# A three-block transformer in fp32: the first stage reordered by need, its norm sums on VectorE, head norms with two root and two square buffers

## The reference

```python
for l in range(2):                                   # first_block
    mod  = silu(c) @ w_ada[l] + b_ada[l]             # six groups of 1024: sh1 sc1 gt1 sh2 sc2 gt2
    modc = silu(c_ctx) @ w_ada[l] + b_ada[l]
    h = rmsnorm(x, g_mix[l]) * (1 + sc1) + sh1       # the same for ctx with modc
    p = h @ w_in[l]
    # q and k heads of 64: rmsnorm of each head, gain, then rotation t*cos + turned(t)*sin
    x = x + gt1 * mixer(...)    # global and windowed attention, short convolution, gates, w_out
    x = x + gt2 * expert_choice_ffn(...)             # 16 experts, each takes its top tokens
# second_block: rmsnorm, q/k/v/gate projections, head norm and rotation, banded and
# dilated causal attention, silu gates, w_out, residual
```

## Time and profile before

| | us |
|---|---|
| median of 3 runs (lowest to highest) | 3480.6 (3479.9 to 3485.0) |
| the profiled execution's own time | 3479.7 |
| its span in the trace | 3477.7 |
| PE busy | 3198.9 (92% of the span) |
| DVE busy / ACT busy | 1075.6 / 641.6 |

### The profile page before, as it was taken

One profiled execution on the slowest core, in us unless ns is written; L12 is line 12 of the kernel. 1 busy time (PEld: TensorE's weight loads), 2 busy tenths in 40 slices (PEclk: granted clock), 3 DMA queues, 4 the chain that ended last, 5 costly groups with the idle time before them and its releaser, 6 DMA issues. The chain is left out here.

```text
span 3477.7 us, 35357 instructions
## 1 busy us (share of the span) xinstructions
PE 3198.9 (92%) x13776; PEld 1568.4 (45%) x13776; DVE 1075.6 (31%) x1541; ACT 641.6 (18%) x1124; POOL 16.7 (0%) x35
## 2 busy tenths in 40 slices
PE   6989999999997999999988999999789889888978
PEld 3565555555553333333343654444423324343544
DVE  2566644555422010101036561011300010036241
ACT  3137500000011111111121560000111101021151
POOL 1000000000000000000000000000000000000000
PEclk8999999999998999999999999999899999999999
DMA  7020033443414878787830201223198988942200
GB/s 222 0 73 1 1 121 115 145 150 105 139 49 154 304 285 307 285 304 289 303 93 0 73 1 55 73 73 103 37 376 346 404 355 352 405 114 49 61 1 25
DMA packets 305434, 551.85 MB, mean 159 GB/s; under 512 B 62744, under 2 KB 145960, under 8 KB 305160
## 3 DMA queue, kind: packets, MB, share of 16 engines
q1 hardware_dynamic: 303376, 546.53, 44.2%
q0 software_dynamic: 1600, 3.20, 0.3%
q10 hardware_dynamic: 312, 0.05, 0.0%
HBM read 547.63 MB, written 2.10 MB: 158 GB/s over the span
## 5 line engine op out<-in xcount | busy, mean ns | idle before, releaser
L736 PE MATMUL ps<-hT,ring 128*128 128x512 f32 (+1 forms) x2576 | 969.6, 534 | 29.5 <-ACT hT L1259 27.7
L736 PEld LDWEIGHTS ps<-hT,ring 128*128 128x128 f32 x2576 | 492.6, 192 | 494.1 <-issue 464.4
L1013 PE MATMUL ps<-ring,hT 128*64 128x512 f32 x1536 | 356.9, 600 | 64.4 <-DMA ring<-in_w_e_up 35.5
L992 PE MATMUL ps<-ring,hT 128*64 128x512 f32 x1536 | 350.8, 598 | 1.5 <-ACT hT L1259 1.5
L1013 PEld LDWEIGHTS ps<-ring,hT 128*64 128x64 f32 x1536 | 100.2, 136 | 311.1 <-issue 159.3
L1906 DVE SCALAR_TENSOR_TENSOR xT<-ps,mod,xT 128x512 f32<-128x512 f32 x96 | 63.5, 662 | 498.7 <-PE ps L1099 281.1
L992 PEld LDWEIGHTS ps<-ring,hT 128*64 128x64 f32 x1536 | 101.8, 136 | 235.6 <-issue 235.1
L736 PE MATMUL ps<-obuf,ring 128*128 128x512 f32 (+1 forms) x512 | 198.5, 540 | 1.3 <-issue 1.3
L998 PE MATMUL ps<-ring,hT 128*32 128x512 f32 x1536 | 184.7, 598 | 0.0
L1591 DVE SCALAR_TENSOR_TENSOR vbuf<-ring,silc,vbuf 128x1024 f32<-128x1024 f32 x140 | 179.9, 1285 | 5.7
L1259 ACT ACTIVATE prob<-ps 128x512 f32<-128x512 f32 (+1 forms) x56 | 38.6, 688 | 673.7 <-PE ps L736 673.7
(11 more groups left out here) (223 smaller groups left out, 2471.0 us busy)
## 6 DMA issues: line engine op xcount, KB each, us to landing
ring<-in_w_e_gate SPq DMA_DIRECT2D x128, 512.0 KB, 7.2
ring<-in_w_e_up SPq DMA_DIRECT2D x128, 512.0 KB, 7.1
ring<-in_w_e_down SPq DMA_DIRECT2D x128, 512.0 KB, 6.9
ring<-in_w_e_gate SPq DMA_DIRECT2D x64, 1024.0 KB, 10.6
ring<-in_w_e_up SPq DMA_DIRECT2D x64, 1024.0 KB, 10.7
ring<-in_w_e_down SPq DMA_DIRECT2D x64, 1024.0 KB, 10.7
ring<-in_w_in SPq DMA_DIRECT2D x49, 1024.0 KB, 5.6
ring<-in_w_ada SPq DMA_DIRECT2D x48, 1024.0 KB, 6.8
```

The costliest lines, as they stand in the source:

```text
L736: mm = pe.matmul(ps[:, b + a:b + e], lhs[:, k, :], rhs[:, k, a:e], start=k == 0, stop=k == nk - 1)
L992: mm = pe.matmul(ps[e * CX:(e + 1) * CX, b + pair * 512:b + (pair + 1) * 512], lhs[:, k, s0:s0 + CX], expert_dst(0, slot, e)[:, k % 2, :], ...
L1013: mm = pe.matmul(ps[e * CX:(e + 1) * CX, b + h * 512:b + (h + 1) * 512], lhs[:, k, s0:s0 + CX], expert_dst(1, slot, 0)[:, e, h * 512:(h + ...
```

## The change

1. SP: the big block of constants (rotation, head and mask tables) is issued after the eight `w_ada` chunks and two `w_in` chunks; the identity matrix stays in front. c and c_ctx have their own small DMAs, first on ACT's queue, and are turned ahead of x.
2. The eight `w_ada` chunks are cut otherwise: 256 rows by 1024 columns in place of 1024 rows by 256 columns. Four chunks make one group: sc1 (`adf` g=1) first, then sh1 (g=0), each copied and turned once.
3. ACT squares each tile of x as soon as it is copied; DVE adds the eight squares up (`add_square`); PE needs one product over 768 columns (job `ns`) in place of eight. Root and reciprocal follow between the two groups.
4. DVE scales by the root alone; the amplitude goes into ACT's shift operation (`scale=`). Both go through the 512 columns of all `d` first, then the 256, in all layers; PE waits for each range apart, and so does the reciprocal.
5. The meetings of all engines in the first stage are gone.
6. Head phase, all layers: two root buffers, two square buffers, a scratch of its own for the rotation, and the rotation one job later.

```diff
-C_ID, C_SUM, C_PICK, C_ROT, C_HEAD, C_MASK, C_IOTA = 0, 128, 130, 134, 262, 390, 390 + 7 * P
+C_ID, C_PICK, C_ROT, C_HEAD, C_MASK, C_IOTA = 0, 128, 136, 264, 392, 392 + 7 * P
...
+        cond = pr[0:2 * KD, 2, 0:P]
+        roots = [rs, pr[:, 1, :]]
+        squares = [sq, pr[:, 2, :]]
+        turn_term = pr[:, 0, 0:NX]
...
                 order.append(j)
-                if rots:
+                if len(rots) > 1:
                     order.append(rots.pop(0))
...
-        FIRST = [(w, 0, n + (w == "ada")) for n in range(-1, 8) for w in ("ada", "adat") if 0 <= n + (w == "ada") < 8]
+        FIRST = [("adf", 0, 1, q) for q in range(4)] + [("ns", 0), ("adft", 0, 1)]
+        FIRST += [("adf", 0, 0, q) for q in range(4)] + [("adft", 0, 0), ("pv", 1)]
...
-            if name == "ada":
-                return plain(w_ada[l], n * CH)
-            if name == "acc":
+            if name in ("adf", "acc"):
...
                     for k in range(nk):
-                        if ph is not None and (ph, k) not in seen_h:
-                            need(h_ready, ph + (k,))
-                            seen_h.add((ph, k))
+                        if ph is not None and (ph, k, a) not in seen_h:
+                            need(h_ready, ph + (k, a))
+                            seen_h.add((ph, k, a))
...
+                elif kind == "ns":
+
+                    pe.wait_ge(first_added, 1)
+                    b = begin(("norm", 0, "mix"))
+                    for a, e in halves(NT):
+                        mm = pe.matmul(ps[:, b + a:b + e], ones[:, :], h3[:, 0, a:e], start=True, stop=True)
+                    part(mm, ("norm", 0, "mix"))
...
+            pe.wait_ge(s_ident, 16)
+            pe.wait_ge(s_cond, 32)
+            b = begin(("cond", 0))
+            part(pe.transpose(ps[:, b:b + 2 * KD], cond, ident[0:2 * KD, 0:2 * KD]), ("cond", 0))
             pe.wait_ge(s_x, 32)
-            pe.wait_ge(s_const, 32)
...
-            sp.dma_start(con[:, 0:C_ROT], consts[:, 0:C_ROT]).then_inc(s_const, 16)
+            sp.dma_start(con[:, 0:C_ROT], consts[:, 0:C_ROT]).then_inc(s_ident, 16)
...
+            for n in range(RING + 4):
+                load(n)
             sp.dma_start(con[:, C_ROT:C_HELD], consts[:, C_ROT:C_HELD]).then_inc(s_const, 16)
-            end = 0
+            end = RING + 4
...
                 elif kind == "qk":
                     w = width(l, j[2])
+                    n = hs_number[("hs",) + j[1:]]
                     b = A.read(j)
-                    if last_hs[0]:
-                        A.read(last_hs[0])
-                    A.do(func(sq[:, 0:w], ps[:, b:b + w], ACT.Square), qsq_ready, j)
-                    last_hs[0] = ("hs",) + j[1:]
+                    if n >= 2:
+                        A.read(hs_of[l][n - 2])
+                    elif l > 0:
+                        A.read(("affT", l - 1))
+                    A.do(func(squares[n % 2][:, 0:w], ps[:, b:b + w], ACT.Square), qsq_ready, j)
                 elif kind == "hs":
-                    A.need(*last_rs[0])
-                    root(j, width(*j[1:]), HD)
-                elif kind == "rot":
-                    last_rs[0] = (q_ready, j)
+                    n = hs_number[j]
+                    if n >= 2:
+                        A.need(qn_ready, hs_of[l][n - 2])
+                    elif n == 0:
+                        A.need(*last_rs[0])
+                    root(roots[n % 2], j, width(*j[1:]), HD)
...
+            turned_x(1)
+            for d in range(3, KD, 2):
+                turned_x(d)
+                V.do(add_square(d - 2))
+                V.do(add_square(d - 1))
+            add_square(KD - 1).then_inc(first_added, 1)
+            dve.wait_ge(first_added, 1)
+            params(0)
...
+            def scaled(ph, a, e, d0, d1):
+                for d in range(d0, d1):
+                    V.do(v.tensor_tensor(h3[:, d, a:e], xT[:, d, a:e], rs[:, a:e], ALU.mult), hpre, ph + (d, a))
...
-                V.do(v.reciprocal(rs[:, 0:w], rs[:, 0:w]))
-                for d in range(KD):
-                    for a, e in halves(w):
-                        ins = v.scalar_tensor_tensor(h3[:, d, a:e], xT[:, d, a:e],
-                                                     amp4[:, ph[0], ph[1] == "ffn", d, a // 512:a // 512 + 1],
-                                                     rs[:, a:e], ALU.mult, ALU.mult)
...
+                for a, e in halves(w):
+                    V.do(v.reciprocal(rs[:, a:e], rs[:, a:e]))
+                    scaled(ph, a, e, 0, KD)
...
+                elif kind == "adft" and j[2] == 1:
+                    modulation_first(j)
+                    scaled((0, "mix"), 0, NX, 0, 2)
+                elif kind == "adft":
+                    modulation_first(j)
+                    scaled((0, "mix"), 0, NX, 2, KD)
+                    V.do(v.reciprocal(rs[:, NX:NT], rs[:, NX:NT]))
+                    scaled((0, "mix"), NX, NT, 0, KD)
```

More of the change, by code:

```diff
@@ L60, in constants @@
     for w in range(2):
-        c[w::32, C_SUM + w] = 1.0
-    for r in range(4):
-        c[32 * r, C_PICK + r] = 1.0
+        for r in range(4):
+            c[32 * r + w, C_PICK + 2 * r + w] = 1.0
     for f in range(P):
@@ L588, in load_params @@
             param(sinks[:, l, :], sink_b[l].partition_broadcast(P))
[L589 to L592, removed]
+            if l == 1:
                 rows(PEXTRA, norm_gain_2[0])
@@ L714, in need, with norm_piece @@
                 pe.wait_ge(ev.sem, ev.at[key])
+            def norm_piece(b, ph, of_, d, w):
+                need(sq_ready, ("n",) + ph + (d,))
+                for a, e in halves(w):
+                    norm_piece.last = pe.matmul(ps[:, b + a:b + e], ones[:, :], of_[:, d, a:e], start=d == 0, stop=d == KD - 1)
             def norm_sum(ph, w):
@@ L720, in norm_sum @@
                 for d in range(KD):
-                    need(sq_ready, ("n",) + ph + (d,))
-                    for a, e in halves(w):
-                        mm = pe.matmul(ps[:, b + a:b + e], ones[:, :], m3[:, d, a:e], start=d == 0, stop=d == KD - 1)
-                part(mm, key)
+                    norm_piece(b, ph, m3, d, w)
+                part(norm_piece.last, key)
             seen_h = set()
@@ L1115, in _ @@
                 part(mm, ("xT", d))
-            for l in range(DEPTH):
-                pe.wait_ge(s_param[l], PARAM_DMAS[l] * 16)
-                b = begin(("pv", l))
-                rows = PROWS[l]
-                part(pe.transpose(ps[:, b:b + rows], prob[0:rows, l, 0:P], ident[0:rows, 0:rows]), ("pv", l))
-            meet()
+            run(("pv", 0))
             for j in FIRST:
@@ L1291, in norm @@
-                for d in range(KD):
-                    A.need(hpre, ph + (d,))
-                    for a, e in halves(w):
-                        shift = zero3[:, d, 0:1] if l == 2 else mod3[:, l, sh + d, a // 512:a // 512 + 1]
-                        ins = func(h3[:, d, a:e], h3[:, d, a:e], ACT.Identity, bias=shift)
-                        if e == w:
-                            A.do(ins, h_ready, ph + (d,))
-                        else:
-                            A.do(ins)
-            last_hs, ada_turned, group_turned = [None], [], []
+                if l > 0:
+                    for d in range(KD):
+                        A.do(func(m3[:, d, 0:w], xT[:, d, 0:w], ACT.Square), sq_ready, ("n",) + ph + (d,))
+                    root(rs, ("norm",) + ph, w, D)
@@ new lines, in norm @@
+                last_rs[0] = (hpre, ph + (KD - 1, halves(w)[-1][0]))
+                A.need(amp_ready, (l, 0))
+                if l < 2:
+                    A.need(ada_done, ("adag", l, SH1 // 8) if l else ("adft", 0, 0))
+                for a, e in halves(w):
+                    for d in range(KD):
+                        A.need(hpre, ph + (d, a))
+                        shift = zero3[:, d, 0:1] if l == 2 else mod3[:, l, SH1 + d, a // 512:a // 512 + 1]
+                        A.do(func(h3[:, d, a:e], h3[:, d, a:e], ACT.Identity, bias=shift,
+                                  scale=amp4[:, l, 0, d, a // 512:a // 512 + 1]), h_ready, ph + (d, a))
@@ L1632, in run @@
                 w = width(l, j[2] if kind in ("qk", "hs") else "")
-                if kind == "adat":
-                    modulation(j)
+                if kind == "ns":
+                    V.need(rms_ready, ("norm", 0, "mix"))
+                    V.do(v.reciprocal(rs[:, 0:NX], rs[:, 0:NX]))
                 elif kind == "acc":
```

204 lines of the change are left out of this document (110 added, 94 removed).

## The result

The changed kernel takes 3393.48 us (median of four, 3392.21 to 3393.85) against 3481.86 for the kernel before on the same chip (3479.89 to 3485.04). The ratio is 0.9745, with a 95% interval of 0.9728 to 0.9762: it is faster. The prediction was 3392, with 3384 to 3408 as its range. The profiled span fell from 3477.7 to 3391.8, by 85.9 us, where the sum said 88.6.

What follows compares the result with a forecast made beforehand. PE was busy 3198.9 of 3477.7 us, so its idle and low-clock time was the gain: 27.1 + 3.5 + 60.4 - 2.4 = 88.6, span 3389.1; plus 2.0 for profiled time and 0.9 for the median: 3392, range 3384 to 3408.

Steps and rivals of the forecast that it cites:

- the sum: Whole kernel: gains of 27.1 + 3.5 + 60.4 - 2.4 = 88.6 us, taking the span from 3477.7 to 3389.1.
- The head phases: Head phases of all layers: PE's waits and clock dips vanish, periods fall to 12.46 and 8.58; gain 60.4 us.
- The first stage: Start of the kernel: first projection at 42.5 instead of 69.64; gain 27.1 us (25.1 to 28.2).
- Rival (c): First stage: chunks with 4 KB rows still land at 348 GB/s, first projection at 44.5, time 3394; chance 0.15.
- rival (a): First stage: the chain through VectorE ends last, first projection at 48, time 3398; chance 0.07.
- The norms: Norms of layer 1 and the second block: projection starts sooner after the norm, gaining 3.4 and 0.1 us.
- (b): Head phases keep part of their wait: period some 9.8 at 512 columns, 20 us less gain, 3412; chance 0.06.
- (d): Head phases: clock at 1.2 GHz for a third loses 90 us and the gain; for half, 3526; slower's chance 0.01.
- (e): Whole change does nothing, since the head phases' turn would wait for something outside `rs`; chance 0.02.
- What is late next: First scores, layers 0 and 1: two turns behind the last value job cost 1.1 to 1.3 each, -2.4; second block nothing.
- a sign of being wrong: Prediction wrong if PE's time in later stages changes, the turn still waits, or the last `w_ada` chunk is used after 40.

Runs made afterwards that it cites:

- neither: Changed kernel with the head phase wholly as before (single buffers, rotation at its old place), keeping the new beginning and norms: 3444.39 us.
- short_rows: Changed kernel with each of the first eight `w_ada` chunks loaded by four DMAs of 1 KB rows instead of one of 4 KB rows: 3398.23 us.
- rot_later_only: Changed kernel with one root buffer, one square buffer and the scratch back in the root buffer; only the rotation stays a job later: 3392.89 us.
- buffers_only: Changed kernel with all the new head-phase buffers but the rotation where it was before: 3385.89 us, and 3388.45 when measured again.
- squares_and_scratch: As buffers_only (rotation where it was), with two square buffers and the rotation's own scratch, but one root buffer: 3387.04 us.
- drained_early: Changed kernel, rotation still later inside the head phase, but all waiting rotations put right behind each value or gate job: 3388.59 us.
- one_square: As buffers_only, but with one square buffer; two roots and the scratch stay: 3421.41 us.
- two_squares_only: As buffers_only, but with one root buffer that is the rotation's scratch too; only the square is double: 3394.25 us.

## Why the prediction was right

The time was forecast to 1.5 us, and part of that is luck. The two parts, as the run neither divides them, missed in opposite directions: the beginning and the norms are worth 35.7 where the sum has 30.6, the head change 50.9 where it has 58.0. The head phases themselves did what was said: in the traces of neither and of the changed kernel they give 10.2 + 22.5 + 24.5 = 57.2 up to the second or third scores. The stretches between them give 3.9 back, and the profiled run of neither was the slowest of its four. The mechanisms held; where the sizes differ is told below, stage by stage.

**The first stage** came out 1.3 us better than its sum (28.4 against 27.1, just above its range of 25.1 to 28.2). The transposes started at 14.29 for 14.6. The last chunk was used at 37.59, inside 36.4 to 39.5, 5.1 earlier than before. The rows gave 2.9 of that: in short_rows the same bytes in rows of 1 KB run at 349 GB/s and end that much later. The constants gave less than the prediction's 3.2: with them in front the last chunk is used 1.2 later (1.1 to 2.0 against all nine kernels with this first stage). The remaining 1.0 wasn't traced. The Trainium skill's page "DMA: Bandwidth & Descriptors" (Specifications) puts the limit of one core at about 358 GB/s. The changed kernel's trace doesn't agree: it shows 407 with one core running, and no run here has two. Rival (c), with nearly the time of that rule, fell with it. VectorE's chain ended at 37.75, not at 39.9: its additions ended at 29.34 (29.1 predicted), but PE's product took 1.56 at full clock, not 2.6, and the steps behind it 37.75 - 30.96 = 6.8, not 8.2. There the prediction had counted ACT's table load between product and root; in the changed kernel it comes earlier, at 27.82, and 1.0 passes from product to reciprocal, not 2.4. So rival (a) fell too: VectorE was done 2.1 before it was needed. An addition of 768 columns took 2.94 / 3 = 0.98 with its gap, where I had taken 1.0 from the copies.

The parts that were tried are worth 2.5 (constants, half of it clock), 2.9 (rows) and 4.5 (sums on VectorE), each taken out alone. They share the end of two chains and needn't add up; that the other 18 or so of 28.4 is the order (squares, sums and root ahead of the modulation instead of behind it) was not tried by itself and is a remainder.

**The norms.** Layer 1 gained 2.4 from the first sum to the projection where 3.4 was said; from there to its first head sum came another 0.7. From reciprocal to projection lay 5.2 us, 5.1 in the prediction. The second block gained 1.6 for 0.1, because PE's sums there took 7.10 in place of 8.80, at a higher clock; no step of the change explains that part.

**The head phases.** The whole difference of the periods came, dips included. From first projection to first scores layer 0 gained 13.8: 10.6 + 1.1 as predicted, 1.4 because the first two jobs took 22.57, not 23.96, and 0.9 for the turn that moved behind the value jobs. Layer 1 gained 24.8: 23.3 as predicted, the 0.7 above and the 0.9. The second block gained 26.7 up to its gates: 25.4 as predicted, the 0.9, and 0.5 because its first job took 9.36, not 9.89. Behind the gates it lost 2.5, hence the 24.2. Rivals (b), (d) and (e) fell: the period is 8.58, the clock 1.00, the wait gone. What the prediction did not say is that it needs only one half of the edit. Its count of a whole job more for the turn was right, and that half alone gives the full time (rot_later_only); the other half alone gives it too, and more.

**The step that was off is "What is late next", and only for the second block.** In layers 0 and 1 the second scores lose 2.0, because PE's wait rose from 2.4 to 4.4, and the moved turn gives 0.86 back in the head phase: 1.2 net in each, as the prediction's 1.1 to 1.3 says. For the second block it put nothing, because gate jobs lie in between. But a rotation waits until another joins it, and none joins it during the gates, so the last turn stands behind them (3223.70), right before the scores. From the start of the gates to the third batch of scores it is 59.95 before (3258.42 to 3318.37) and 62.38 in the changed kernel (3168.77 to 3231.15): 2.4 later, 1.6 net of the moved turn. Of this 0.4 isn't the turn's, for buffers_only, which has no turn there, needs 60.39; 1.1 is. In all the three places cost 1.2 + 1.2 + 1.6 = 4.0 where the sum has 2.4.

Taking that step back where it hurts makes a better kernel than the changed one: buffers with the rotation in its old place (3385.9 and 3388.5), squares_and_scratch (3387.0) and drained_early (3388.6), all 5 to 8 us below 3393.5. Each of their ranges of times ends below the changed kernel's lowest run, 3392.21, though the intervals of the ratios overlap. Of these 5 to 8 the places above explain only about 2 to 3, net of the moved turn and of short waits in the head phase. From projection to second scores the lead of buffers_only grows by 0.1 in layer 0 (its first two jobs took 23.92, at a lower clock, for 22.57) and in layer 1 from 1757.70 - 1753.23 = 4.5 to 5.2, by 0.7; in the second block it grows by 1.2 up to the third scores. For drained_early the same three are 0.5, 1.1 and 1.3. Most of the rest lies in stretches of lower clock, which fell otherwise in the two traces; whether the late turns cause that was not shown.

**The rest of the way from 88.6 to 85.9** between sum and span lies mostly in the clock. Between the scores of layer 0 and the norm of layer 1 the gain shrinks from 40.2 to 37.8: PE is busy 1.4 us more and idle 1.0 more for the same work. A wait of 1.39 at the router (L960, at 999.10) is new, but it costs nothing: the transposes ahead of it took 3.60 in the kernel before and take 1.97 now, and VectorE sets the time there. Between the scores of layer 1 and the norm of the second block the gain shrinks by 1.6, all of it busy time. The prediction had named a change of PE's time in later stages as a sign of being wrong; there is one, but a small one. One part can be seen in windows of the same product, first of the changed kernel, then of the one before:

```profile
895.00:911.00 16.00, 15.48 (x43) 8.44 (x44) 3.58 (x12) 0.84 (x1) 0.00 (x0) 0.89 0.36 126
```

```profile
935.00:950.00 15.00, 14.01 (x43) 7.95 (x44) 4.05 (x12) 0.84 (x1) 0.00 (x0) 1.00 0.40 140
```

The product of `merged` with `wout` took 12.25 us in the changed kernel (from 895.52), 10.56 in the one before (from 935.99) and 10.56 in buffers_only (from 893.90), behind a wait of 1.02 or 1.03 in all three. That is 1.7 us lost to a dip that the code at this place doesn't explain. The end of the second block loses 1.2 in the same way (clock 0.91 from 3275 to 3293, where the counterpart before had 1.00).

## What to carry to other kernels

When a chain of latencies over three engines sets a loop's period, look for the one resource that closes the ring. Here a second square buffer alone was worth some 50 us of the 57 that all the buffers gave; beside it the scratch for the rotation was worth about 7, and a second root nothing. Putting the reader a job later opens the same ring without any memory, but it leaves a tail; the tail has to be drained before the next stage's first use. In a stage where everybody waits, write down each chain with its own end: here the norm's chain ended at 37.75 and the chunks' chain at 39.87, so by estimate more work taken off the chunks' chain alone would pay for 2.1 us at most.

## What the runs showed of the hardware

- Longer rows loaded faster from HBM: with one core running, the same 1 MB chunks came at 349 GB/s in rows of 1 KB and at 407 in rows of 4 KB. One or four DMAs for a chunk made no difference (348 and 349 at 1 KB).
- A wait costs PE more than its length. In one_square 1.29 us of waiting made the period 1.56 longer: of the 0.27, 0.1 is in the turn (1.12 for two products that take 1.02 without a wait); the rest is that without a wait the turn starts 0.16 before the projection's end, as in two_squares_only, where it starts at 1806.61 after a projection from 1799.74 of 7.03. The kernel before has the same in layer 0: 1.24 us of waiting in each job, and 13.97 - 12.46 = 1.51 more a job.
- The clock stayed at 1.00 in 76 us of head phase without a pause. With a wait in every job it didn't always: 0.98 in one_square from 1783 to 1869, where the two products behind a wait of 3.15 took 1.99, not 1.12. Its 25.5 us of waiting cost 33 to 36; its 24 waits at 0.27 more each are some 6 of the difference, by estimate, and the rest is clock and the spread of the runs.
- Which of two equal places meets a dip of the clock differs from kernel to kernel (895.52 above), so a difference of 2 us at one place need not come from an edit there.
